# Stick-breaking attention: key-block sums formed by GpSimd before the products with ones, and the first two key blocks in one triangle product

## What is computed

```python
def stick_breaking(q, k, v, bias, q_offset):
    """A[t,s] = sigmoid(z_ts) * prod_{s<j<t} (1 - sigmoid(z_tj)), s < t strictly; log space."""
    z = jnp.einsum('bqhd,bkhd->bhqk', q, k) * (HD_B ** -0.5)
    z = z + bias[None, :, None, None]
    mask = jnp.arange(Lk)[None, :] < (q_offset + jnp.arange(Lq))[:, None]
    u = jnp.where(mask, jax.nn.log_sigmoid(-z), 0.0)
    rev_excl = lax.cumsum(u, axis=3, reverse=True) - u
    A = jnp.where(mask, jnp.exp(jax.nn.log_sigmoid(z) + rev_excl), 0.0)
    return jnp.einsum('bhqk,bkhd->bqhd', A, v)
```

## Time and profile before

| what | value |
|---|---|
| median of 3 runs | 1504.93 us |
| the profiled execution's own time | 1504.54 us |
| its span in the profile | 1502.8 us |
| TensorE matmul busy | 1482.4 us (99%) |
| VectorE busy | 1179.4 us (78%) |
| ScalarE busy | 824.5 us (55%) |
| GpSimd busy | 325.4 us (22%) |
| share of L3349 (`later_sums`) in the chain that ended last | 2.7% |

### The profile page before, as it was taken

How to read it: one execution, slowest core, us unless ns; L and a number is a source line. 1 busy time by engine, 2 the same in 40 slices (tenths; PEclk the granted TensorE clock), 3 DMA queues, 4 the chain that set the end, 5 groups by cost and what they waited for, 6 DMA issues and landing times.

```text
span 1502.8 us, 33760 instructions
## 1 busy us (share of the span) xinstructions
PE 1482.4 (99%) x13024; PEld 1406.3 (94%) x13024; DVE 1179.4 (78%) x1999; ACT 824.5 (55%) x1296; POOL 325.4 (22%) x314
## 2 busy tenths in 40 slices
PE   8999999999999999999999999999999999999998
PEld 8999999989999999999998888888799999999998
DVE  7866666667998988989835888888779989898753
ACT  6544444436654635546523777777756546364543
POOL 3000000002332232322142121112243332332221
PEclk9999999999999999999999999999999999999999
DMA  6233333223777777777435555543338778677621
GB/s 191 58 87 88 87 87 87 87 87 87 162 159 171 162 162 179 155 155 170 114 99 177 189 188 185 180 156 113 101 85 165 179 155 182 155 160 181 143 85 64
DMA packets 237716, 205.83 MB, mean 137 GB/s; under 512 B 8268, under 2 KB 224404, under 8 KB 237588
## 3 DMA queue, kind: packets, MB, share of 16 engines
q1 hardware_dynamic: 151346, 147.34, 31.3%
q0 software_dynamic: 68160, 47.20, 20.5%
q10 hardware_dynamic: 18082, 9.48, 2.3%
HBM read 192.19 MB, written 11.80 MB: 136 GB/s over the span
## 4 chain that ended last, share of the span: by engine, by line
PE 93%; DVE 4%; issue 1%; ACT 1%; DMA 0%; DVEq 0%; ACTq 0%
PE acc L2868 22%; PE acc L3191 18%; PE pL L3191 12%; PE pM L3191 9%; PE acc L3291 6%; PE pO L3191 3%; PE pM L3349 3%; PE pL L2989 1%; PE pO L3363 1%; PE pL L3332 1%; PE acc L3129 1%; PE acc L3406 1%; PE pO L3395 1%; PE acc L3423 1%; PE pM L3058 1%
## 5 line engine op out<-in xcount | busy, mean ns | idle before, releaser
L652 POOL TENSOR_TENSOR wlo<-wraw,whi 128x512 fp32r<-128x512 f32 x40 | 56.1, 1434 | 461.5 <-ACT whi L777 461.5
L2868 PE MATMUL acc<-xa_hi,whi 128*128 128x288 f32 x544 | 124.9, 311 | 0.2 <-DVE hT L2328 0.2
L863 ACT ACTIVATE hi<-wraw 128x1024 fp32r<-128x1024 f32 x60 | 63.7, 1062 | 104.3 <-DVE wraw L1998 104.3
L846 ACT ACTIVATE hi<-wraw 128x1024 fp32r<-128x1024 f32 x60 | 63.7, 1061 | 103.1 <-PE acc L3191 102.8
L2868 PE MATMUL acc<-xa_hi,wlo 128*128 128x288 f32 x544 | 116.5, 296 | 0.0
L2868 PE MATMUL acc<-xa_lo,whi 128*128 128x288 f32 x544 | 116.0, 295 | 0.0
L3191 PE MATMUL acc<-X_lo,hi 128*128 128x288 f32 x384 | 113.3, 295 | 0.0
L3191 PE MATMUL acc<-X_hi,lo 128*128 128x288 f32 x384 | 113.3, 295 | 0.0
L3191 PE MATMUL acc<-X_hi,hi 128*128 128x288 f32 x384 | 113.1, 295 | 0.0
L2013 DVE TENSOR_TENSOR lo<-wraw,hi 128x1024 fp32r<-128x1024 f32 x60 | 73.3, 1221 | 42.2 <-ACT hi L846 42.2
L3191 PE MATMUL acc<-H_hi,hi 128*128 128x288 f32 x336 | 99.3, 296 | 1.3 <-DVE lo L2019 1.3
(11 more groups left out here) (547 smaller groups left out, 5150.4 us busy)
## 6 DMA issues: line engine op xcount, KB each, us to landing
wraw<-in_w_up_dram SPq DMA_DIRECT2D x64, 512.0 KB, 6.1
wraw<-in_w_down_dram SPq DMA_DIRECT2D x64, 512.0 KB, 5.1
Kp<-in_cache_k_dram SPq DMA_DIRECT2D x32, 512.0 KB, 4.2
Vp<-in_cache_v_dram SPq DMA_DIRECT2D x32, 512.0 KB, 5.4
wraw<-in_w_in_a_dram SPq DMA_DIRECT2D x30, 512.0 KB, 5.4
wraw<-in_w_up_dram POOLq DMA_DIRECT2D x32, 256.0 KB, 4.7
S_even<-in_w_up_dram POOLq DMA_DIRECT2D x32, 256.0 KB, 5.9
S_odd<-in_w_up_dram POOLq DMA_DIRECT2D x32, 256.0 KB, 6.9
```

Of the source, the lines that this page charges most:

```text
L652: ins = pool.tensor_tensor(wlo[s][:, k:k + 2, :], wraw[s][:, k:k + 2, :], whi[s][:, k:k + 2, :].bitcast(F32), ALU.subtract)
L846: act.activation(blocks4(hi02), by_rows(G % 2)[:, 0], ACT.Copy).then_inc(piece_hi, 1)
L863: act.activation(blocks4(hi31), by_depth(G % 2)[:, 0], ACT.Copy).then_inc(piece_hi, 1)
L2868: last = pe.matmul(acc[a][:, hf, 0:HALF], w[s][:, k, a * P:(a + 1) * P], x[k][:, hf * HALF:(hf + 1) * HALF], start=(k == 0 and n == 0), st ...
```

## The change

For a head, the products with ones of group 1 were over block 2 and block 3, and those of group 2 over blocks 1, 2 and 3. The ones matrix sums over all keys of a block, so the blocks can be added to each other first. After the change:

- GpSimd adds block 3 to the last 128 columns of block 2 (`later_sum_1`, 128x128), and adds that to the last 256 columns of block 1 (`later_sum_0`, 128x256). Both are done in float32 in tl, before splitting into parts.
- ScalarE takes the high parts of the two sums (`later_high_1`, `later_high_0`) and VectorE the low parts (`later_low_1`, `later_low_0`). They overwrite their columns in uh and ul once `later_sums` of the group before has read them.
- `later_sums` has 4 products in each step: two triangle products over the whole group (in group 0 both blocks in one, 384 columns) and two with ones, of 128, 256 and 384 columns in groups 0, 1 and 2. It waits for u_lo once ahead of the triangle and once ahead of the ones.
- The tiles tl are six, one for each n, and `softplus` no longer waits for a free one; kf has lost the zeroed columns behind its end, and one product of `new_rows` writes 64 partitions in place of 128.
- GpSimd makes bias_neg of the next pair between the sums (`turn_sums`), after the last logits of a pair have been read, as before.

```diff
--- before.py
+++ after.py
@@ -172,21 +172,27 @@
         GROUPS = [[(3, 0), (2, 128)], [(1, 0)], [(0, 0)]]
         GCOL, GW = [0, 384, 768], [384, 384, 512]
         UOFF = {3: 0, 2: 128, 1: 384, 0: 768}
+        LATER = [slice(0, 128), slice(128, 384), slice(384, 768)]
+        S1_COLS, S0_COLS, N_U = slice(256, 384), slice(512, 768), 10
+        H_AT, S1_HI = (1, 2, 3, 4, 7, 9), (5, 6)
+        LATER_AT = (1, 2, 4, 6, 8, 10)
+        U_AT, S0_HI = (1, 2, 4, 5, 7, 9), (8, 10)
...
 
@@ -742,20 +748,43 @@
                                    bias_h[:, bass.ds(2 * j, 2)].rearrange("p (h a) -> p h a", a=1).to_broadcast([P, 2, P]),
                                    ALU.add).then_inc(bias_ready, 1)
 
+
+            def later_sum_1(j, hh):
+
+                pool.wait_ge(u_lo, N_U * j + U_AT[hh])
+                pool.tensor_tensor(tl[hh][:, S1_COLS], tl[hh][:, S1_COLS], tl[hh][:, 0:P], ALU.add).then_inc(bias_ready, 1)
+
+            def later_sum_0(j, hh):
+
+                pool.wait_ge(u_lo, N_U * j + U_AT[2 + hh])
+                pool.wait_ge(bias_ready, 5 * j + 2 + hh)
+                pool.tensor_tensor(tl[2 + hh][:, P:3 * P], tl[2 + hh][:, P:3 * P], tl[hh][:, P:3 * P], ALU.add
+                                   ).then_inc(bias_ready, 1)
+
+            def turn_sums(j):
+                later_sum_1(j, 0)
+                kv_low(j + 2, 0)
+                later_sum_1(j, 1)
+                masked_bias(j + 1)
+                later_sum_0(j, 0)
+                later_sum_0(j, 1)
+
             kv_low(0, 0)
             kv_low(0, 1)
             kv_low(1, 0)
             pool.wait_ge(unit_done, U_OB)
             masked_bias(0)
             kv_low(1, 1)
-            with pool.Fori(1, NPAIR - 1) as j:
-                kv_low(j + 1, 0)
-                masked_bias(j)
-                kv_low(j + 1, 1)
-            kv_low(NPAIR, 0)
-            masked_bias(NPAIR - 1)
+            with pool.Fori(0, NPAIR - 2) as j:
+                turn_sums(j)
+                kv_low(j + 2, 1)
+            turn_sums(NPAIR - 2)
             pool.wait_ge(hi_done, U_OB // 2)
             split_low_unit(1).then_inc(lo_done, 1)
+            later_sum_1(NPAIR - 1, 0)
+            later_sum_1(NPAIR - 1, 1)
+            later_sum_0(NPAIR - 1, 0)
+            later_sum_0(NPAIR - 1, 1)
             pool.wait_ge(lo_done, U_OB // 2 + 1)
             split_low_panel(1, U_OB // 2 + 1)
             split_low(U_OB // 2 + 2, U_MLP1 // 2)
@@ -1405,14 +1434,25 @@
             def softplus(j, n):
                 g, hh = divmod(n, 2)
                 act.wait_ge(B_free[hh], 4 * j + 2 + g)
-                wait(act, u_lo, 6 * j + n - 3)
-                soft3(Am[hh][:, GCOL[g]:GCOL[g] + GW[g]], tl[n % 4][:, 0:GW[g]], 18 * j + 3 * n, soft)
+                soft3(Am[hh][:, GCOL[g]:GCOL[g] + GW[g]], tl[n][:, 0:GW[g]], 18 * j + 3 * n, soft)
 
             def u_high(j, n):
                 g, hh = divmod(n, 2)
                 act.wait_ge(sp_done, 6 * j + n + 1)
                 wait(act, R_full, 7 * j)
-                act.activation(uh[hh][:, GCOL[g]:GCOL[g] + GW[g]], tl[n % 4][:, 0:GW[g]], ACT.Copy).then_inc(u_hi, 1)
+                act.activation(uh[hh][:, GCOL[g]:GCOL[g] + GW[g]], tl[n][:, 0:GW[g]], ACT.Copy).then_inc(u_hi, 1)
+
+            def later_high_1(j, hh):
+
+                act.wait_ge(bias_ready, 5 * j + 2 + hh)
+                act.wait_ge(R_full, 7 * j + hh + 2)
+                act.activation(uh[hh][:, S1_COLS], tl[hh][:, S1_COLS], ACT.Copy).then_inc(u_hi, 1)
+
+            def later_high_0(j, hh):
+
+                act.wait_ge(bias_ready, 5 * j + 5 + hh - (isinstance(j, int) and j == NPAIR - 1))
+                act.wait_ge(R_full, 7 * j + hh + 4)
+                act.activation(uh[hh][:, S0_COLS], tl[2 + hh][:, P:3 * P], ACT.Copy).then_inc(u_hi, 1)
 
             def weights(j, n):
                 g, hh = divmod(n, 2)
@@ -1445,15 +1485,19 @@
                 weights_in(0)
                 u_high(j, 3)
                 t_copy(j + 1, 4)
+                later_high_1(j, 0)
                 softplus(j, 4)
                 t_copy(j + 1, 6)
                 softplus(j, 5)
+                later_high_1(j, 1)
                 past_soft(j + 1)
                 u_high(j, 4)
+                later_high_0(j, 0)
                 weights(j, 0)
                 weights(j, 1)
                 weights(j, 2)
                 u_high(j, 5)
+                later_high_0(j, 1)
                 k_high(j + 1)
                 past_weights(j + 1)
                 weights(j, 3)
@@ -2556,7 +2604,7 @@
                 dve.wait_ge(B_full, 8 * j + n + 3)
                 wait(dve, AV_full, j)
                 if g == 0:
-                    dve.wait_ge(bias_ready, j + 1)
+                    dve.wait_ge(bias_ready, 1 if isinstance(j, int) and j == 0 else 5 * j - 1)
                 nd = len(GROUPS[g])
                 c0, c1, c2 = GCOL[g], GCOL[g] + nd * P, GCOL[g] + GW[g]
                 dve.scalar_tensor_tensor(out=Am[hh][:, c0:c1].rearrange("p (b t) -> p b t", t=P),
@@ -2567,7 +2615,7 @@
 
             def sp_add(j, n):
                 g, hh = divmod(n, 2)
-                tv = tl[n % 4][:, 0:GW[g]]
+                tv = tl[n][:, 0:GW[g]]
                 dve.wait_ge(soft, 18 * j + 3 * n + 3)
                 dve.wait_ge(B_free[hh], 4 * j + 2 + g)
                 dve.scalar_tensor_tensor(out=tv, in0=Am[hh][:, GCOL[g]:GCOL[g] + GW[g]], scalar=0.0, in1=tv, op0=ALU.max,
@@ -2576,9 +2624,21 @@
             def u_low(j, n):
                 g, hh = divmod(n, 2)
                 cols = slice(GCOL[g], GCOL[g] + GW[g])
-                dve.wait_ge(u_hi, 6 * j + n + 1)
+                dve.wait_ge(u_hi, N_U * j + H_AT[n])
                 dve.wait_ge(sp_done, 6 * j + n + 1)
-                dve.tensor_tensor(ul[hh][:, cols], tl[n % 4][:, 0:GW[g]], uh[hh][:, cols].bitcast(F32), ALU.subtract
+                dve.tensor_tensor(ul[hh][:, cols], tl[n][:, 0:GW[g]], uh[hh][:, cols].bitcast(F32), ALU.subtract
+                                  ).then_inc(u_lo, 1)
+
+            def later_low_1(j, hh):
+
+                dve.wait_ge(u_hi, N_U * j + S1_HI[hh])
+                dve.tensor_tensor(ul[hh][:, S1_COLS], tl[hh][:, S1_COLS], uh[hh][:, S1_COLS].bitcast(F32), ALU.subtract
+                                  ).then_inc(u_lo, 1)
+
+            def later_low_0(j, hh):
+
+                dve.wait_ge(u_hi, N_U * j + S0_HI[hh])
+                dve.tensor_tensor(ul[hh][:, S0_COLS], tl[2 + hh][:, P:3 * P], uh[hh][:, S0_COLS].bitcast(F32), ALU.subtract
                                   ).then_inc(u_lo, 1)
 
             def minus_later(j, n):
@@ -2678,19 +2738,23 @@
                 minus_later(j, 0)
                 t_copy(j + 1, 5)
                 logits_in(j, 5)
+                later_low_1(j, 0)
                 t_copy(j + 1, 7)
                 minus_later(j, 1)
                 u_low(j, 2)
                 past_logits(j + 1)
                 u_low(j, 3)
                 sp_add(j, 4)
+                later_low_1(j, 1)
                 minus_later(j, 2)
                 sp_add(j, 5)
                 past_sp(j + 1)
                 u_low(j, 4)
                 minus_later(j, 3)
+                later_low_0(j, 0)
                 past_later(j + 1)
                 u_low(j, 5)
+                later_low_0(j, 1)
                 minus_later(j, 4)
                 past_AT(j + 1)
                 k_low(j + 1)
@@ -2764,7 +2832,6 @@
...
@@ -3315,7 +3382,7 @@
             def new_rows(j):
                 pe.transpose(pM[0:SMP, 0:P], kf[:, SEQ:T], ident[:])
                 pe.transpose(pM[0:SMP, P:2 * P], vf[:, SEQ:T], ident[:])
-                pe.matmul(pM[:, 2 * P:3 * P], kf[:, SEQ:SEQ + P], qnew[:].rearrange("p h t -> p (h t)"), start=True, stop=True
+                pe.matmul(pM[0:SMP, 2 * P:3 * P], kf[:, SEQ:T], qnew[:].rearrange("p h t -> p (h t)"), start=True, stop=True
                           ).then_inc(R_full, 1)
 
             def logits(j, g):
@@ -3340,15 +3407,17 @@
                 if n == 0:
                     pe.wait_ge(N_free, j + 1)
                     pe.wait_ge(n_dve, 6 * j + 1)
-                pe.wait_ge(u_lo, 6 * j + n + 1)
-                for kb, c0 in GROUPS[g]:
-                    for k2 in range(kb, NCH):
-                        w = SEQ - k2 * P
-                        c = c0 + (k2 - kb) * P
-                        for u in (uh[hh], ul[hh]):
-                            last = pe.matmul(pM[:, c:c + w], (tri_r if k2 == kb else ones_r)[:],
-                                             u[:, UOFF[k2]:UOFF[k2] + w], start=(k2 == kb and u is uh[hh]),
-                                             stop=(k2 == NCH - 1 and u is ul[hh]))
+                pe.wait_ge(u_lo, N_U * j + U_AT[n])
+                tri = slice(GCOL[g], GCOL[g] + GW[g])
+                for u in (uh[hh], ul[hh]):
+                    pe.matmul(pM[:, 0:GW[g]], tri_r[:], u[:, tri], start=u is uh[hh], stop=False)
+                pe.wait_ge(u_lo, N_U * j + LATER_AT[n])
```

(6 more changed lines are left out.)

14 lines of the change are left out of this document (7 added, 7 removed).

## The result

The changed kernel takes 1510.25 us (median of 7 runs, 1507.47 to 1512.32), the kernel before, run beside it, 1504.9 us (7 runs, 1503.63 to 1505.99). The ratio is 1.0034, 95% interval 1.0024 to 1.0044: slower. The forecast was 1506.5 us and no change, the range ended at 1509.5. The profiled execution took 1511.05 us, with a span of 1508.1. Of the 6.5 us by which it lies above the one before (1504.54), 5.3 are in the span and 1.2 outside it.

A forecast was written before the change was run, and what follows sets the result against it. TensorE was 99% busy, but VectorE's row of work, with 0.63 us idle, was taken to decide. 1504.54 - 0.35 (seven pairs) + 1.96 (last pair) = 1506.15 us profiled, median 1506.5, no change; range 1500.5 to 1509.5.

The forecast's parts named there:

- the hold by GpSimd in the last pair: Last pair: GpSimd's two large additions run beside VectorE instructions with two SBUF inputs and hold VectorE for 0.80 us.
- The steady pair: Each pair before the last: 33.96 us before the change, forecast to gain 0.05 us; seven pairs, -0.35 us.
- VectorE's three subtractions: Steady pair, ahead of the reading of step 4's sums: added `later_low` work of 0.21 + 0.34 + 0.34 = 0.89 us.
- The port: Steady pair: GpSimd's last addition holds the shared SBUF port, so `later_low_1(1)` on VectorE waits; taken as 0.40 us.
- the walk: Steady pair: VectorE's work followed to the reading of step 4's sums: 946.20 - 0.63 - 0.03 + 0.89 + 0.40 = 946.83.
- The pair gains 0.05 us: TensorE's 1.36 us turn into waits for VectorE: Steady pair: removed products save TensorE 1.36 us, but `later_sums(5)` waits for VectorE's reading of pM; 0.05 us gained.
- The last pair costs +1.96 us: Last pair: VectorE is the chain; its instruction before the last sums comes 2.37 us later, those sums are 0.41 shorter.
- The wait for ScalarE: Last pair: `later_low_1(0)` needs its high part from ScalarE, so VectorE waits 0.47 us.
- the shorter last sums: Last pair, TensorE: the last `later_sums` was to be 0.41 us shorter.
- The port kept by VectorE: Rival: GpSimd's additions wait instead; a steady pair gains 0.45 us, the last costs 1.16: 1502.9 us, chance 0.25.
- The columns come back: Rival: VectorE's extra work finds room, a pair gains 1.26 us, the last 0.4: 1495.7 us, chance 0.10.
- Slower: the port stops VectorE more often than once a pair: Rival: further GpSimd additions also hold VectorE (0.2 and 0.4 us), each pair costs 0.55 us: 1510.8 us, chance 0.15.

The follow-up runs named there:

- number 2: Changed kernel with the product of `new_rows` made wide again (128 columns of weights): 1507.05 us, ratio 1.0017 to the kernel before.
- number 9: Changed kernel with the wide product of `new_rows` and GpSimd's four additions cut to 8 columns, VectorE's order as in the change: 1502.87 us, ratio 0.9988.
- number 12: Changed kernel with the wide product of `new_rows`, and GpSimd's additions and VectorE's `later_low` subtractions all cut to 8 columns: 1496.3 us, ratio 0.9944.
- number 1: Kernel before with one edit of the change alone, the narrowed product of `new_rows`: 1506.61 us, ratio 1.0013.
- number 7: Changed kernel with the wide product of `new_rows` and, in the last pair alone, each `later_low` behind the `minus_later` it preceded: 1505.28 us, ratio 1.0006.

## Why the prediction was wrong

Two terms failed: the narrowed product of `new_rows`, which the prediction put at nothing without a reason, and the hold by GpSimd in the last pair, which was sized too small. A fall of TensorE's clock behind its holes had no term at all.

**The steady pair: right, but for a product that was left out.** The forecast's 33.91 us is measured at 33.96 with the wide product (number 2), and that kernel's 1507.05 us lies in the range, below the 1507.9 from which the prediction speaks of slower. The terms, one by one:

- VectorE's three subtractions stand 0.22, 0.33 and 0.33 us in the row in number 9, for 0.21, 0.34 and 0.34.
- The port was set at 0.40 us and is 0.54 (numbers 2 and 9). It didn't show in the walk because the instruction before the reading then stands in a dense row (0.60 us from start to start, its duration of 0.69 was counted) and a gap of 0.04 us closed: 8.35 us for 8.31. That errors of 0.14 and 0.13 us cancelled is luck.
- "The pair gains 0.05 us: TensorE's 1.36 us turn into waits for VectorE": with both of VectorE's burdens gone (number 12), TensorE gains 1.16.

What failed is the list of what the change adds and removes: it speaks of `later_sums` alone on TensorE. The narrowed product of `new_rows` was in the diff and I gave it no line. It costs 0.28 us per pair (number 1), 2.2 us in eight (1.94 by the medians of number 1), and it alone takes the forecast of 1506.5 to 1508.7, past the 1507.9 of "slower". The trace of before held a warning: at 918.80, where products with 64 columns of weights give way to products with 128, the weight load stops for 0.17 us. It would have been no sure price, since the transposes of the same form don't stop it.

**The last pair: mechanism right, size too small.** "The last pair costs +1.96 us"; it cost 2.73. The reading of step 4's sums (1079.66) comes 2.96 us later against the pair's start than in the earlier trace rows, where 2.37 was forecast. Of the 0.59 between, 0.3 is the narrow product, which is outside the forecast's list as above, and the rest the port: it holds VectorE for 0.56 + 0.52 = 1.08 us, not 0.80. The wait for ScalarE moves the row by the 0.47 foretold. Then came what no step had: after TensorE's holes the clock fell. The reading of 1079.66 ends at 1080.35, but `later_sums(5)` starts only at 1080.73, some 0.33 us later than it could, since the three products of the output projection ahead of it still take 1.31 us (1079.42 to 1080.73; the like three at 1076.81 in number 7 take 0.69). And from its start to the product with the values it is 3.06 us, for 3.62 before: 0.56 shorter, where I took 0.41. So 2.96 + 0.33 - 0.56 = 2.73.

**In sum.** Narrow product 2.2, last pair's port 0.3, clock 0.3, less 0.15 for the shorter last sums: about 2.7 us of the 3.75 between forecast and median. The other 1.0 us is not settled, but the runs show where most of it lies: outside the span. The kernel before has 1.70 to 1.88 us of its time there in all 83 runs of the three sessions, number 1 1.70 to 1.80, the changed kernel 1.87 to 2.95 in its 7 runs, 2.65 in the median: 0.9 us more. The kernels derived from it reach up to 2.96 in single runs. What brings it is open.

**The rivals.** The port kept by VectorE (1502.9): refuted by the mean of 621 ns; the case of the earlier trace rows in which VectorE went on unharmed was the exception. The columns come back (1495.7): not in this kernel, but number 12 shows that the price was nearly right: 1496.3 us, 8.4 under the kernel before, where the rival had 9.2. "Slower: the port stops VectorE more often than once a pair" (1510.8): its time nearly came out, its reason is wrong. In the steady pair the large additions held VectorE once, and the first small one, at 937.62, cost about 0.13 in a gap.

## What to carry to other kernels

When columns are taken from a full engine, walk the next engine's row of work between two waits and count its idle time: that walk came within 0.05 us a pair here, in part by luck. Where GpSimd has to work beside VectorE, put a VectorE instruction with an input in PSUM where the addition will fall, and let a subtraction that nobody waits for yet stand behind the reading that frees a bank: two exchanged lines per place were worth 0.46 and 0.30 us a pair. And give every line of the diff a price, the smallest product too: one that looks like a saving of half the weights cost 2.2 us here, more than the whole change that was forecast (1.6).
